# Eight modulation slabs summed by VectorE, the context fetched later, and two expert slabs loaded early

## The reference

```python
mod_x = (silu(c) @ w_ada + b_ada)          # six vectors of 1024: sh1, sc1, gt1, sh2, sc2, gt2
mod_c = (silu(c_ctx) @ w_ada + b_ada)      # the same for the context: csh1, csc1 are used
h  = rms_norm(x, g_attn)   * (1 + sc1)  + sh1
hc = rms_norm(ctx, g_attn) * (1 + csc1) + csh1
qa, ka, va, qb, kb, vb = split_projection(h @ w_qkv)      # keys and values of hc come before those of h
lat_mix = concat([gqa_attention(qa, ka, va), diff_attention(qb, kb, vb, lam)])
x = x + gt1 * (lat_mix @ w_o)
h = rms_norm(x, g_ffn) * (1 + sc2) + sh2
logits = h @ w_router + b_router           # top 4 of 32, softmax over the 4
y = sum over the chosen e of gate[e] * (swiglu(h @ w_in[e] + b_in[e]) @ w_out[e] + b_out[e])
x = x + gt2 * y
```

## Time and profile before

| | us |
|---|---|
| median of 3 runs | 2231.81 (2229.91 to 2232.53) |
| the profiled execution, as timed | 2230.88 |
| its span | 2229.0 |
| TensorE busy | 2077.0 (93%) |
| VectorE busy | 541.4 (24%) |
| ScalarE busy | 409.1 (18%) |
| mean rate of the DMA engines | 282 GB/s |

### The profile page before, as it was taken

The page is one execution under the profiler, slowest core; times in us unless marked ns, Lnnn a source line. Parts: engine busy times, 40 slices in busy tenths (PEclk is TensorE's granted clock), DMA queues, the critical chain, the costliest instruction groups (busy, mean ns, idle before and its releaser), DMA issues.

```text
span 2229.0 us, 25264 instructions
## 1 busy us (share of the span) xinstructions
PE 2077.0 (93%) x10358; PEld 1337.0 (60%) x10358; DVE 541.4 (24%) x1156; ACT 409.1 (18%) x771; POOL 174.7 (8%) x225
## 2 busy tenths in 40 slices
PE   6999879999899899899999999999999998989998
PEld 4644654444444333444444458488788888878887
DVE  1065332212222111222221243113102404510321
ACT  3124211111111111111111120312113205320211
POOL 0000000000000000000000000000291951000000
PEclk9999979999999999999999999999999999999999
DMA  9539829999999999999999996445343342534320
GB/s 362 193 143 387 337 79 417 417 417 417 417 418 418 417 418 418 418 418 418 417 402 407 418 393 239 157 156 204 136 147 142 142 161 94 197 124 155 120 106 19
DMA packets 164372, 627.79 MB, mean 282 GB/s; under 512 B 5232, under 2 KB 9456, under 8 KB 127824
## 3 DMA queue, kind: packets, MB, share of 16 engines
q1 hardware_dynamic: 163840, 625.39, 71.7%
q0 software_dynamic: 464, 1.44, 0.2%
HBM read 625.76 MB, written 1.05 MB: 281 GB/s over the span
## 4 chain that ended last, share of the span: by engine, by line
PE 73%; DMA 15%; DVE 7%; ACT 2%; issue 2%; SPq 1%; DVEq 0%; ACTq 0%
PE psum L920 31%; PE psum L1217 22%; DMA ring<-in_w_in_dram 13%; PE psum L931 2%; PE psum L955 2%; PE psum L1193 2%; PE psum L1237 2%; DVE arena L2170 1%; PE psum L1304 1%; PE psum L1105 1%; PE psum L1477 1%; DMA ring<-in_w_ada_dram 1%; DVE arena L2185 1%; DMA ring<-in_w_o_dram 1%; SPq L802 1%
## 5 line engine op out<-in xcount | busy, mean ns | idle before, releaser
L1217 PE MATMUL psum<-ring,arena 128*64 128x512 f32 x3168 | 712.1, 607 | 79.6 <-DMA ring<-in_w_in_dram 78.7
L920 PE MATMUL psum<-arena,ring 128*128 128x256 f32 (+1 forms) x3072 | 684.0, 385 | 6.1 <-ACT arena L1552 6.1
L920 PEld LDWEIGHTS psum<-arena,ring 128*128 128x128 f32 x3072 | 586.0, 191 | 102.0 <-issue 21.8
L1217 PEld LDWEIGHTS psum<-ring,arena 128*64 128x64 f32 x3168 | 240.1, 140 | 537.9 <-issue 483.0
L1668 ACT ACTIVATE arena<-psum 128x512 f32<-128x512 f32 (+1 forms) x155 | 88.6, 571 | 835.2 <-PE psum L1217 712.4
L2170 DVE TENSOR_TENSOR arena<-psum,arena 128x512 f32<-128x512 f32 (+1 forms) x68 | 44.3, 672 | 430.2 <-PE psum L1237 430.2
L2157 DVE TENSOR_SCALAR arena<-consts,arena 128x64 f32<-128x64 f32 (+1 forms) x68 | 16.7, 310 | 338.3 <-PE psum L1217 338.3
L2425 DVE SCALAR_TENSOR_TENSOR consts<-psum,smalls,consts 128x255 f32<-128x255 f32 (+1 forms) x88 | 38.4, 478 | 233.1 <-ACT consts L1811 232.3
L2572 POOL DMA_DIRECT2D arena<-in_pos_dram x1 | 0.6, 579 | 1037.0 <-DVE tiny L2249 1037.0
L1588 ACT ACTIVATE arena<-psum 128x512 f32<-128x512 f32 (+1 forms) x56 | 31.6, 566 | 259.2 <-PE psum L920 183.5
L1193 PE MATMUL psum<-arena 128*128 128x256 f32 x288 | 70.3, 387 | 4.4 <-DVE arena L2146 3.4
(11 more groups left out here) (346 smaller groups left out, 1563.4 us busy)
## 6 DMA issues: line engine op xcount, KB each, us to landing
ring<-in_w_in_dram SPq DMA_DIRECT2D x132, 2048.0 KB, 15.1
ring<-in_w_out_dram SPq DMA_DIRECT2D x66, 2048.0 KB, 18.0
ring<-in_w_ada_dram SPq DMA_DIRECT2D x36, 2048.0 KB, 14.0
ring<-in_w_up_dram SPq DMA_DIRECT2D x22, 2048.0 KB, 7.9
ring<-in_w_ret_dram SPq DMA_DIRECT2D x12, 2048.0 KB, 12.5
ring<-in_w_down_dram SPq DMA_DIRECT2D x16, 1408.0 KB, 6.0
ring<-in_w_qkv_dram SPq DMA_DIRECT2D x4, 2048.0 KB, 18.8
ring<-in_w_rout_dram SPq DMA_DIRECT2D x4, 2048.0 KB, 9.4
```

The source lines that it names most:

```text
L920: ins = nc.tensor.matmul(bank(c)[:, at:at + n], w[:, k, m * P:m * P + P], r, start=(k == 0), stop=(k == k_tiles - 1))
L1217: ins = nc.tensor.matmul(psum[at:at + CAP, p, :], act[:, k, CAP * e:CAP * e + CAP], w[:, kk, n0:n0 + BANK], start=(k < 3 - halves), stop=( ...
```

## The change

Seven edits, all to the first block:

- **Order at the start.** The load of the context moves behind the slab `qa`. The norm of the context is taken by TensorE between the two halves of qa's product, by ACT behind `scale_and_shift(1)` and by DVE behind the first modulation.
- **Sums by DVE.** The eight remaining ada slabs (`SUMMED`) are loaded among the projections' slabs. DVE multiplies each slab's eight tiles by the condition and adds them up; `summed_rows` lets TensorE sum the partitions with eight matmuls before vb's last tile. ACT copies the rows once (`copy_rows(2)`), so groups 1 and 2 are one. Attention keeps the 12 ada2 slabs, in steps of `[1, 1, 1, 0]`.
- **w_o.** All tiles have their first part done before the wait, with the second part behind it.
- **Router.** Its weights get a place of their own at the arena's end and are loaded at the first rope. ACT takes the exp of the top values before the copies of tokens.
- **b_out.** Its product goes behind the first gather, into PSUM banks 4 to 7, and DVE's memsets and copies behind the first selection.
- **Early slabs.** The second double slab of the first pair's `w_in` goes into free places of the arena (`early_w`), the first half when attention has ended, the second when the tokens have been copied; the first pair is taken out of the loops.
- **Turns.** `turn_h` and the gates of a pair are transposes in place of products with the identity.

```diff
-STEP_SLABS = [2, 1, 1, 1] * 4
+STEP_SLABS = [1, 1, 1, 0] * 4
+SUMMED = MOD_KEYS[4:12]
...
-    chunk(("norm", 1), ("norm", 0))
+    chunk(("norm", 1))
     for key in MOD_KEYS[:4]:
         slab(key, 0)
     chunk(("cols", 0))
-    slab("qa", 2)
+    chunk(("qa", 0), ("norm", 0), ("qa", 1))
+    slabs["qa"] = len(chunks)
     slab("kva", 2)
+    for key in SUMMED[:2]:
+        slab(key, 0)
     slab("qb", 2)
+    for key in SUMMED[2:5]:
+        slab(key, 0)
     slab("kb", 4)
+    for key in SUMMED[5:]:
+        slab(key, 0)
...
+        w_rt = arena[:, ARENA - KD * E:].rearrange("p (a b) -> p a b", b=E)
+        at = KD * T + TT * D + KD * T + KD * P
+        early_w = [arena[:, at:at + SLAB].rearrange("p (a b) -> p a b", a=UP_TILES), (flat(h_moe), flat(sq))]
...
-            sp.dma_start(ctx_x, cT.rearrange("(k p) t -> p k t", p=P)).then_inc(ctx_in, 16)
...
+                if n == 4:
+                    sp.dma_start(ctx_x, cT.rearrange("(k p) t -> p k t", p=P)).then_inc(ctx_in, 16)
...
-            for j in range(12):
-                if j < RING:
-                    slab_left(sp, SLAB_KEYS[SLABS_1 + j - RING])
+            for q in range(12 - EARLY_SLABS):
+                j = q if q < 2 else q + EARLY_SLABS
+                if q == 4:
+                    read_ready(sp, ("ob", 3))
+                    sp.dma_start(early_w[0], expert_source(0, 1)).then_inc(early_in[0], 16)
+                if q == RING:
+                    read_ready(sp, ("htok", 3))
+                    for kk, out in enumerate(early_w[1]):
+                        sp.dma_start(out, expert_source(1, 1)[:, kk, :]).then_inc(early_in[1], 16)
+                if q < RING:
+                    slab_left(sp, SLAB_KEYS[SLABS_1 + q - RING])
                 else:
-                    sp.wait_ge(moe.rows_done, (j - RING) // 2 + 1)
-                load(SLABS_1 + j, expert_source(j % 2, j // 2))
+                    sp.wait_ge(moe.rows_done, 1 if q < 8 else 3)
+                load(SLABS_1 + q, expert_source(j % 2, j // 2))
...
+            def summed_rows():
+                pe.wait_ge(mod_summed, len(SUMMED))
+                for n in range(len(SUMMED)):
+                    q = n % 4
+                    nc.tensor.matmul(psum[32 * q:32 * q + 32, ROWS_BANK[2], :], unit[:, 7 - n:39 - n],
+                                     mod_sums[n // 4][:, n % 4, :], start=(n < 4), stop=(n >= 4)
+                                     ).then_inc(rows_used, 1)
...
-            for m in (0, 2):
+            for m in range(4):
                 wo_tile(0, m, 0, 4)
...
             for n in range(2):
-                for m in (0, 2):
+                for m in range(4):
                     wo_tile(n, m, 4, KD)
-                    wo_tile(n, m + 1, 0, KD)
...
             gather(moe, 2, 1)
+            pe.wait_ge(bout_in, 16)
+            copied(pe, ("gates", 0))
+            for k in range(KD):
+                ins = nc.tensor.matmul(psum[:, 4 + k // 2, T * (k % 2):T * (k % 2) + T],
+                                       b_out_sb[0:E, k * P:k * P + P], gates_t[0:E, :], start=True, stop=True)
...
+            dve.wait_ge(normed_ready, 8)
+            for n, key in enumerate(SUMMED):
+                dve.wait_ge(ring_full[SLOT[key]], FULL[key])
+                w, out = slab(key), mod_sums[n // 4][:, n % 4, :]
+                own.link(V.tensor_scalar(out, w[:, 0, :], cond32[:, 0, 6:7], None, ALU.mult))
+                for k in range(1, KD):
+                    ins = V.scalar_tensor_tensor(out=out, in0=w[:, k, :], scalar=cond32[:, k, 6:7], in1=out,
+                                                 op0=ALU.mult, op1=ALU.add)
...
+            pool.wait_ge(q_ready, 1)
+            pool.dma_start(w_rt, w_router.rearrange("(k p) n -> p k n", p=P)).then_inc(router_in, 16)
             pool.wait_ge(x_ready, 1)
-            pool.dma_start(w_rt, w_router.rearrange("(k p) n -> p k n", p=P)).then_inc(router_in, 16)
```

More of the change, by code:

```diff
@@ L230, in plan @@
     take_turns(2, 3)
-    ended = []
+    ended = [2]
     for t in range(STEPS):
@@ L244, in plan @@
     chunk(("norm", 2), ("router", 0), ("htok", 0), ("htok", 1), ("htok", 2), ("htok", 3), ("pos", 0),
-          ("gates", 0), *(("bout", i) for i in range(4)))
+          ("gates", 0))
     before_loop = len(slabs)
@@ L305, in places @@
     for n in range(SLABS_1 + MOE_SLABS):
-        loads[n % RING] += 1
+        loads[slot_at(n)] += 1
         if n < SLABS_1:
-            slot[SLAB_KEYS[n]], full[SLAB_KEYS[n]] = n % RING, 16 * loads[n % RING]
-    queue = [((SLABS_1 + n) % RING, None) for n in range(RING)]
+            slot[SLAB_KEYS[n]], full[SLAB_KEYS[n]] = slot_at(n), 16 * loads[slot_at(n)]
+    queue = [(slot_at(MOE_0 + n), None) for n in range(RING)]
     held = []
@@ L575, in transformer_blocks_kernel @@
         over_ready = sem("over_ready")
+        bout_ready = sem("bout_ready")
+        early_in = [sem(f"early_in{n}") for n in range(2)]
+        bout_read = sem("bout_read")
         pos_ready = sem("pos_ready")
@@ L975, in _ @@
             modulation_cols(0)
-            features("qa", lambda k: h_all[:, k, T:N_KEYS], 2, first=h_tiles(1))
+            features("qa", lambda k: h_all[:, k, T:N_KEYS], 2, first=h_tiles(1), within=lambda: norm(0))
             pe.wait_ge(h_ready, 16)
@@ L1161, in _ @@
             for c in range(4):
-                begin(("bout", c))
-                if c == 0:
-                    pe.wait_ge(bout_in, 16)
-                    copied(pe, ("gates", 0))
-                for m in range(2):
-                    k = 2 * c + m
-                    ins = nc.tensor.matmul(half(("bout", c), m), b_out_sb[0:E, k * P:k * P + P],
-                                           gates_t[0:E, :], start=True, stop=True)
-                end(ins)
-            for c in range(4):
-                copied(pe, ("bout", c))
+                copied(pe, ("htok", c))
+            copied(pe, ("pos", 0))
             def gather(s, halves, n):
@@ L1196, in scatter, with experts @@
                     ins.then_inc(s.x_ready, 1)
-            def experts(s, halves, i, full, ring_slot):
+            def experts(s, halves, i, full, tile):
                 width = CAP * halves
@@ L1251, in experts @@
                 for t in range(TT):
-                    ins = nc.tensor.matmul(psum[:, 2, t * P:t * P + P], gsel[:, t, :],
-                                           con("ident"), start=True, stop=True)
+                    ins = nc.tensor.transpose(psum[:, 2, t * P:t * P + P], gsel[:, t, :], con("ident"))
                 ins.then_inc(s.gates_turned, 1)
@@ L1950, in _ @@
             norm(1)
-            norm(0)
             modulation(0)
@@ L2031, in _ @@
                 modulation(group)
-            for group in range(1, 6):
+            for group in range(2, 6):
                 copied(dve, ("cols", group))
@@ L2119, in _ @@
             copied(dve, key)
-            for c in range(4):
-                key = ("bout", c)
-                read_ready(dve, key)
-                read_done(V.tensor_copy(y_moe[:, 2 * c:2 * c + 2, :], two(bank(key))), key)
-            for c in range(4):
-                copied(dve, ("bout", c))
             def one(e):
@@ L2213, in _ @@
             for c in range(2):
+                dve.sem_inc(moe.y_copied, 1)
+            for c in range(4):
+                dve.wait_ge(bout_ready, c + 1)
+                V.tensor_copy(y_moe[:, 2 * c:2 * c + 2, :], two(psum[:, 4 + c, :])).then_inc(bout_read, 1)
+            dve.wait_ge(bout_read, 4)
+            for c in range(2):
                 dve.sem_inc(moe.x_free[c], 1)
-            for c in range(2):
-                dve.sem_inc(moe.y_copied, 1)
-            select(moe, 2, (0, 1), 0)
+            experts(moe, 2, 0, (0, 1), 0, (2, 3), 0)
             for b in range(1, BLOCKS):
```

127 lines of the change are left out of this document (91 added, 36 removed).

## The result

| | before | after |
|---|---|---|
| median of the timed runs, us | 2232.17 (4 runs, 2229.91 to 2235.74) | 2206.32 (4 runs, 2204.84 to 2216.06) |
| profiled execution, us | 2230.88 | 2205.38 |
| its span, us | 2229.0 | 2203.2 |
| q's product done, kva starts | 54.31 | 56.12 |
| scores(0) | 146.26 | 151.63 |

The ratio after to before is 0.9892, 95% interval 0.986 to 0.9924. The forecast was 2206.7 us.

What follows compares the result with a forecast made beforehand. The weight stream at 417 GB/s was taken to bound the expert stage, leaving its late start to gain: −20.1 before the first pair's product, −2.5 early slabs, −2.5 transposes, −25.1 from 2231.8 to 2206.7 us; range 2198 to 2220.

Steps and rivals of the forecast that it cites:

- kva: Start of kva's product behind q's: near 56.1 instead of 54.5, +1.7 us, bounds −2.7 to +6.
- scores(0), with kva and the summed rows: Start of attention: near 150 instead of 146, from kva's +1.7 and the summed rows' +1.9 us on TensorE.
- attention: Eight of 20 slabs leave, but steps with values stay at 6.52 us: −9.6 with w_o's 0.2, bounds −4 to −15.6.
- w_o: From w_o's first matmul to the norm behind it: 33.6 instead of 38.4 us, −4.8, bounds −3.5 to −5.5.
- norm to the router's end: Router: the 5.48 us wait for its weights goes, the h tiles are next in line; −0.9, 0 to −4.
- router's end to S (exp and b_out): Exp ahead of the token copies −1.1 us; b_out's product behind the gather −7.3, range −4.0 to −8.
- S: Start of the first expert pair's product: 300.6 us forecast, 320.72 before.
- Its other bound: The w_o term's smaller size, −3.5 us, at 0.2365 us a matmul, from 96 matmuls containing a half-clock start.
- Early slabs: First pair: two slabs in the arena save only what free slots allow, −2.5 us, −1.6 to −3.9, not −10.
- Transposes: Expert pairs: 1.7 us less a pair, mostly hidden by the stream; −1.7 in pairs, −0.8 in tail, −2.5 together.
- all counts: Rival: TensorE binds attention (−15.6), early slabs worth 10 in full, router warm; 2191 us, 2199 likelier; chance 0.12.
- chains bind more: Rival: attention gives 4, b_out stays cold, early slabs 1.6, pairs and tail 0; 2219 us; chance 0.18.

Runs made afterwards that it cites:

- 5: Changed kernel with one more multiply-add a slab on DVE, into a scratch tile; median 2207.65 us, ratio 0.989 to the kernel before.
- 6: Changed kernel with seven more multiply-adds a slab on DVE, into a scratch tile; median 2242.17 us, ratio 1.0038 to the kernel before.
- 7: Changed kernel with attention's same twelve slabs in steps of 2, 0, 1, 0; median 2219.98 us, ratio 0.9945 to the kernel before.
- 4: Changed kernel with w_o by halves of the outputs again, as before; median 2214.58 us, ratio 0.9916 to the kernel before.
- 8: Changed kernel with the router's weights ordered behind x again, as before; median 2208.39 us, ratio 0.989 to the kernel before.
- 3: Changed kernel with b_out's product and DVE's copies of it ahead of the gather again; median 2214.8 us, ratio 0.9925 to the kernel before.
- 1: Changed kernel without early slabs, all 12 of the first pair through the ring; median 2213.41 us, ratio 0.9908 to the kernel before.
- 2: Changed kernel with products with the identity in place of the pairs' transposes; median 2220.0 us, ratio 0.9939 to the kernel before.
- the filled kernel: `both` with eight matmuls into an unread spare bank behind scores(0) and in steps 3, 7 and 11; median 2203.9 us, ratio 0.9873.
- both: Changed kernel with the context first in the queue, its norm ahead of q's product, and slabs 2 and 8 as early ones; 2207.2 us, ratio 0.9879.

## Why the prediction was right

By its own steps, on the profiled executions:

| step | forecast | measured |
|---|---|---|
| kva | +1.7 | +1.8 |
| scores(0), with kva and the summed rows | +3.6 | +5.4 |
| attention | −9.6 | −9.0 |
| w_o | −4.8 | −5.3 |
| norm to the router's end | −0.9 | −0.7 |
| router's end to S (exp and b_out) | −8.4 | −11.9 |
| S | 300.6 | 299.24 |
| first pair, S to the last up product of pair 1 | −2.5 | −0.8 |
| from there to the last such product | −1.7 | −1.8 |
| tail of the stage | −0.8 | −1.3 |
| rest | 0 | −0.5 |
| sum (span) | −25.1 | −25.8 |

*Kva and scores(0).* Kva came out within 0.1, by two errors that cancel. The norm ended at 48.3 where 47.6 was forecast: q's product began 0.6 earlier than forecast, but its first half took 9.23, not half of 15.6. The chain from there to kva took 7.8, not 8.5. With kva at 54.2 to 56.5 in kernels that are the same up to there, 0.1 is luck besides. Scores(0) was 1.8 too early in the forecast. It had kb in "near 86 (TensorE wants it at 86)"; kb's product began at 85.35, but TensorE was free at 84.21 and stood 1.14. The rest is in differences of under 0.3. The rows took 1.92, as priced. That VectorE's 49 us cost nothing is shown by 5, its price beyond the slack by 6.

*Attention.* That a step with values is held at 6.5 by ScalarE's chain, whatever TensorE has to do, was the main reading, and the 2.49 of idle time at 177.00 is it. Counting slabs alone would have said 14.8. By steps, 4, 8 and 12 gave 1.6, 1.2 and 1.2, as forecast, and step 0 gave 0.9 for 1.5. What the forecast didn't hold is that this length has a second value, 5 us longer, on the clock: at 90.7 the term would have been −4. 7 shows that where the slabs stand is worth 5.0 us by the steps alone, over half of what the eight that left are worth.

*w_o.* Right in mechanism: by 4, 3.5 us are work moved under the wait. The size is luck in part. At the 34.8 us of ten of the twelve kernels the term is −3.6, not the −5.3 of this execution or the −4.8 of the forecast. Its other bound, −3.5 at 0.2365 a matmul, comes out at −3.8 by its own numbers (7.1 + 12.3 + 15.1 against 38.4), and that is about what the kernels do as a rule.

*Router's end to S.* The mis-sized term. The gather was forecast to begin 5.95 us behind the router's end (302.6 less 1.1 for the exp, less 295.55) and began 5.85 behind it, so the chain of exp and masks was right. The 3.5 that were missed lie behind it: gather and b_out took 7.4 together, and the forecast had 10.8, the old 6.88 from gather to S and 3.9 for b_out. It took b_out at 3.9 warm, which it was (3.72), but left the gather at its old price of 6.00; it ran warm too, in 3.81. That is 2.2. Another 0.9 is the old wait for ScalarE between gather and S (0.88), which b_out now covers. Why the gather was warm isn't shown: the wait in front of it fell from 4.10 to 0.84, but in 8 it took 5.44 behind the same 0.84, and in 3 5.29 behind 3.24; in all the other changed kernels it took 3.81.

*Early slabs.* Their worth of 2.5 was right (2.65 by 1), for the reason given: empty slots, not bytes, set the next pair. By 2, though, 1.7 us of that stretch go if the transposes are taken back, where the forecast's −2.5 had no part for the transposes: what was measured belongs to the two edits together. The pair still gained only 0.8, because the first up product ran half cold (8.76 for 7.09): the granted clock was 0.56 over 300 to 303, and 0.63 in the same place in 1. Before, it ran at full clock (44 matmuls in 9.66). In 3, 5 and 8 it took 7.09, and there the last up product of pair 1 stands at S + 78.4 to 78.9, 2.4 to 2.8 before the old S + 81.2: the forecast's 2.5. The forecast had no term for the cold product. It lies against the warm gather; in 3 and 8 the gather was cold and this product warm, in 5 both were warm.

*Transposes.* −3.1 for −2.5, shared as said. Experiment 2 gives 3.7 by the pairs, with the 1.7 of the first one. Neither "all counts" (2191 or 2199) nor "chains bind more" (2219) came: the first would have needed the early slabs at 10 and the attention at −15.6, the second an attention at −4.

The errors left were of both signs (−3.5 at the gather, +1.8 at scores(0), +1.7 in the first pair), and their sum is 0.7. The steps were measured on an execution with the short attention and the warm w_o; the execution of 8 has 4.7 and 1.7 us more there for the same code. And after's own runs spread over 11 us. That the total came within 0.4 us is luck beyond the steps.

## What to carry to other kernels

When slabs leave a pipeline, first name what each step is held by: a step at the length of another engine's chain returns nothing, and where the remaining slabs are put can be worth half as much as how many went. Loads done early pay only as far as slots for their successors are free; ask what the queue does in the time won. And where one kernel's runs spread by 5 us for the same code, compare the granted clock in short stretches before believing a single edit's median, and compare a remedy with the same kernel without it: the filled kernel looks like a cure only until it is set beside `both`.

## What the runs showed of the hardware

- The granted clock of TensorE behind an idle stretch of 2.5 us is not one thing: the same values behind the same 2.49 us took 2.91 in one kernel and 1.95 in another, and the attention 90.7 or 85.8. The 64 matmuls of w_o behind the same 3.5 us took 15.77 in ten kernels and 14.08 in two. With eight matmuls more in each gap the clock was at 2.4 GHz in the one execution seen, and without them it was so in one of `both`.
- VectorE's multiply-add with three operands in SBUF took 752 ns for 128x512 where the DMA engines moved 387 GB/s (after, 90 to 109 us), and the same in the kernel before in a stretch where they moved 1 GB/s: loads into the ring didn't slow it. From the trace of before:

```profile
125.06 0.75 DVE L1975 SCALAR_TENSOR_TENSOR arena<-arena,smalls,sq 128x512 f32<-128x512 f32 x1
120.00:130.00 10.00, 9.34 (x26) 4.53 (x25) 9.48 (x15) 0.60 (x1) 0.00 (x0) 1.00 0.00 1
```
